# Up-bias table folded over both halves of the partitions: pairs of 64-row matmuls instead of 128-row ones

## The chip, the cores and the metric

The kernel runs on one core of one Trainium2 chip. The metric is the device time of one execution in microseconds (us). Before the change it is 1502.85 us, the median of 3 runs (1502.51 to 1503.81). One further execution was taken by the profiler. It took 1498.58 us, and all rows below are from it.

## The reference

One layer of a hybrid decoder over 512 prompt rows and 32 sample rows (544 tokens of 1024 features): a pooling and gating mixer, then a mixture of experts, then a gated input embedding and a last norm. The change touches the mixture of experts only, and in it the two biases:

```python
logits = (x @ w_router + b_router).astype(jnp.float32)
top_logit, top_idx = lax.top_k(logits, TOP_K)          # 4 of 32 experts
...
def expert_block(args):
    xe, e = args                                       # 128 rows, one expert
    gu = xe @ w_up[e] + b_up[e]                        # 1024 -> 2048
    glu = jnp.minimum(gu[:, :D_FF], SWIGLU_LIMIT)
    lin = jnp.clip(gu[:, D_FF:], -SWIGLU_LIMIT, SWIGLU_LIMIT)
    act = glu * jax.nn.sigmoid(SWIGLU_ALPHA * glu) * (lin + 1.0)
    return act @ w_down[e] + b_down[e]                 # 1024 -> 1024
```

`b_up` is 32 experts by 2048, `b_down` 32 by 1024.

## The kernel before

The program is written out engine by engine, with semaphores between the engines and no scheduler: the order on each engine is the order of the code. It has three stages. The first (to about 249 us) does the mixer, the router and the tables. The second is a loop over experts, one step per expert block of 128 rows. The third (from about 1394 us) adds the expert rows, does the embedding gate and the last norm.

In the expert loop each step reads 12 MB of weights: 8 chunks of `w_up` and 4 of `w_down`, 1 MB each, through a ring of 6 buffers (`raw`) that SP fills. The arithmetic is in float32r, and accuracy comes from splitting: ACT copies each chunk to a rounded high part (`w_hi`, line 822), DVE subtracts to get the low part (`w_lo`, line 1466), and TensorE multiplies high by high, high by low and low by high. So each chunk is 12 matmuls of 128 rows by 512 columns: 8 in `hi_products` (line 1161) and 4 in `lo_products` (line 1170).

The biases are added by TensorE as well, in `bias` (line 1151), which opens each accumulation. The table `bias_hl` holds for each expert the high part of its bias in partition e and the low part in partition 32+e; columns 0 to 2047 are `b_up`, 2048 to 3071 are `b_down`, and partitions 64 to 127 are zero. The stationary operand (`oh_up` or `oh_dn`, 128 by 128) is one in the two partitions of the step's expert and zero elsewhere. It comes from `bias_row`, which holds the expert number that each partition stands for. A matmul of the two writes the bias into all 128 rows of PSUM. The up bias is 4 matmuls of 512 columns (`up_start`, line 1181), the down bias 2 (`dn_start`, line 1207). Both stand between matmuls that use all 128 rows: the up bias between the last `lo_products` of the step before and the first `hi_products` of `w_up`; the down bias between a `lo_products` and the first `hi_products` of `w_down`.

The table is made once, in the first stage: 4 DMAs from ACT's queue into `bias_raw` (lines 773 and 774), ACT's copy (line 783), DVE's subtraction (line 1460) and POOL's clearing of partitions 64 to 127 (line 653). TensorE waits for it before the first `x_transposes` of the loop.

Of the kernel before, what the change touches and what calls it, by code (L numbers as in the profile page):

```python
# [22 lines left out]
F32 = mybir.dt.float32  # L23
F32R = mybir.dt.float32r
I32 = mybir.dt.int32
U32 = mybir.dt.uint32
ALU = mybir.AluOpType
ACT = mybir.ActivationFunctionType
AX = mybir.AxisListType

P = 128
# [9 lines left out]
def build(nc, x_prompt, x_sample, state_pool, p_prompt, p_sample, norm_mix, w_in, w_pool, pool_scale,  # L41
# [3 lines left out]
    SEQ, D = x_prompt.shape[1:]  # L45
# [13 lines left out]
    E = w_router.shape[2]  # L59
    FF = w_down.shape[2]  # L60
# [17 lines left out]
    with ctx:  # L78
        def sb(name, shape, dt=F32, scope=ctx):
            return scope.enter_context(nc.sbuf_tensor(name, shape, dt))  # L80

        def sem(name):
            return ctx.enter_context(nc.semaphore(name))
# [19 lines left out]
        bias_row = sb("bias_row", [P, 1])  # L103
# [1 line left out]
        with ExitStack() as s:  # L105
            xTh = sb("xTh", [P, KD, T], F32R, scope=s)
        with ExitStack() as s:
            bias_hl = sb("bias_hl", [P, 2 * FF + D], F32R, scope=s)
        gate_hi3 = sb("gate_hi3", [P, 2, D], F32R)
        junk_t = sb("junk_t", [P, D])  # L110
        x_rows = sb("x_rows", [P, D])
# [3 lines left out]
        with ExitStack() as s:  # L115
            xTl = sb("xTl", [P, KD, TT * P], F32R, scope=s)
        with ExitStack() as s:
            bias_raw = sb("bias_raw", [P, 2 * FF + D], scope=s)
        ple = sb("ple", [P, TT, D])
        with ExitStack() as s:  # L120
            w_v_sb = sb("w_v_sb", [P, KD, SG], scope=s)
# [95 lines left out]
        with ExitStack() as s:  # L217
# [12 lines left out]
            oh_up = sb("oh_up", [P, P], F32R, scope=s)  # L230
            oh_dn = sb("oh_dn", [P, P], F32R, scope=s)
# [45 lines left out]
        JOBS += [(("over", 0), "V"), (("ple", LAST), "A")]  # L277
        assert TT == 5 and all(n % 4 != 3 for n in range(len(JOBS) - 2, len(JOBS)))
        JOB = {name: n for n, (name, _) in enumerate(JOBS)}
        EMPTIED = {}  # L280
        for n, (name, who) in enumerate(JOBS):
            EMPTIED[name] = sum(w == who for _, w in JOBS[:n + 1])
        TOTAL = {who: sum(w == who for _, w in JOBS) for who in "AV"}

        s_job = sem("job_filled")
        s_emptied = {"A": sem("job_emptied_act"), "V": sem("job_emptied_dve")}

        def bank(name, b=0):
            return ps[:, 2 * (JOB[name] % 4) + b, :]
# [12 lines left out]
        def job_filled(eng, name):  # L302
            eng.wait_ge(s_job, JOB[name] + 1)

        ld = {n: sem("ld_" + n) for n in (
            "gain w_v w_z w_u small pool_w state sgu ln w_out gain2 router bias ple p gain_f w_out2 w_out3".split())}
        s_x = [sem(f"ld_x_{t}") for t in range(TT)]
        s_ident = sem("ident_made")
        s_const = sem("constants_made")
# [21 lines left out]
        s_bias_hi = sem("bias_hi")  # L331
        s_bias = sem("bias_table")
# [50 lines left out]
        gu = ps[:, 0:4, :].rearrange("p a b -> p (a b)")  # L383
        dn = ps[:, 4:6, :].rearrange("p a b -> p (a b)")
# [180 lines left out]
        def _(pool):  # L565
            chain = [0]

            def link(ins):
                chain[0] += 1
                ins.then_inc(s_pchain, 1)  # L570
                pool.wait_ge(s_pchain, chain[0])
# [41 lines left out]
            for rest in range(NS, P, NS):  # L613
# [2 lines left out]

            link(pool.iota(bias_row[:], pattern=[[0, 1]], base=0, channel_multiplier=1,
                           allow_small_or_imprecise_dtypes=True))
            link(pool.tensor_scalar(bias_row[E:2 * E, :], bias_row[E:2 * E, :], float(E), None, ALU.subtract))
            pool.tensor_scalar(bias_row[2 * E:P, :], bias_row[2 * E:P, :], 1000.0, None, ALU.add).then_inc(s_const, 1)  # L620
            pool.wait_ge(s_const, 13)

            for t in range(TT):
# [6 lines left out]
            for g in range(G):  # L630
# [7 lines left out]
                for i in range(g + 1):  # L638
                    dst = (sumA, sumB)[(g - i) % 2]
                    sh = 1 << i  # L640
                    lo = (2 << i) - 1
# [8 lines left out]
            pool.memset(x_rows[:], 0.0).then_inc(s_xzero, 1)  # L650
            pool.wait_ge(s_xzero, 1)
            pool.wait_ge(s_sum, G)
            pool.memset(bias_hl[2 * E:P, :].bitcast(F32), 0.0).then_inc(s_bias, 1)
            pool.wait_ge(s_bias, 1)

            pool.wait_ge(s_sum, G)
            for t in range(TT):
# [49 lines left out]
        def _(act):  # L707
# [62 lines left out]
            act.wait_ge(s_mix, 2 * G)  # L770
            act.wait_ge(s_out, 16 * STORES)
            for i in range(2):
                act.dma_start(bias_raw[i * E:(i + 1) * E, 0:2 * FF], b_up[0]).then_inc(ld["bias"], 16)
                act.dma_start(bias_raw[i * E:(i + 1) * E, 2 * FF:], b_down[0]).then_inc(ld["bias"], 16)

            def square2(t):
                act.wait_ge(s_emptied["V"], EMPTIED[("out", t)])
# [1 line left out]
                act.activation(junk[:], resid[:, t, :], ACT.Square, accum_out=sq2[:, t:t + 1]).then_inc(s_sq, 1)  # L779

            def bias_high():
                act.wait_ge(ld["bias"], 64)
                act.activation(bias_hl[0:2 * E, :], bias_raw[0:2 * E, :], ACT.Copy).then_inc(s_bias_hi, 1)

            def p_transposed(t):
                job_filled(act, ("pT", t))
# [133 lines left out]
        def _(pe):  # L920
# [90 lines left out]
            for g in range(G):  # L1011
# [11 lines left out]
                for t in range(LAST):  # L1023
                    pe.matmul(bank(name)[:, t * P:(t + 1) * P], v_sb[:, t, g * P:(g + 1) * P], wsT[:, g, :], start=True, stop=True)
                pe.matmul(bank(name, 1)[:, 0:NS], v_sb[0:NS, LAST, g * P:(g + 1) * P], block_w[0:NS, g, :],
                          start=True, stop=True).then_inc(s_job, 1)
# [16 lines left out]
            for i in range(TT + 2):  # L1043
                if i < TT:
# [3 lines left out]
                    for ks in w_z_halves:  # L1048
                        for b in range(2):
                            for k in range(ks.start, ks.stop):  # L1050
                                if i == 0 and b == 0:
# [4 lines left out]
                                    if k == 3 * KD // 4:  # L1056
# [4 lines left out]
                                               skip_group_check=True)  # L1061
# [45 lines left out]
            for k in range(TOPK):  # L1107
                pe.wait_ge(s_picks, k + 1)
                for t in range(TT):
                    mm = pe.matmul(bank(name)[:, 0:E], picks[:, k % 2, t, :], chosen_row[:, t, k, :],  # L1110
                                   start=(k == 0 and t == 0), stop=(k == TOPK - 1 and t == LAST))
# [34 lines left out]
                    mm = pe.transpose(tp[:, k * P:(k + 1) * P], lin[:, k * P:(k + 1) * P], ident[:])  # L1146
                mm.then_inc(s_atp, 1)

            def bias(out, oh, lo, hi):
                for c in range(lo, hi, 512):  # L1150
                    pe.matmul(out[:, c - lo:c - lo + 512], oh[:], bias_hl[:, c:c + 512], start=True, stop=False,  # L1151
                              skip_group_check=True)

            def hi_products(J, s, out, parts):

# [18 lines left out]
            def up_start(u):  # L1174
                pe.wait_ge(s_xhi, u + 1)
                pe.wait_ge(s_xlo, u + 1)
                pe.wait_ge(s_oh, u + 1)
                if not (isinstance(u, int) and u == 0):
                    pe.wait_ge(s_lin, u)
                    pe.wait_ge(s_glu, u)  # L1180
                bias(gu, oh_up, 0, 2 * FF)

            def up_args(c):
                return gu, [(xT_hi[:, c, :], xT_lo[:, c, :], 0, 2 * FF)]
# [16 lines left out]
            def dn_start(u):  # L1201
                pe.wait_ge(s_ahi, u + 1)
                pe.wait_ge(s_alo, u + 1)
                pe.wait_ge(s_oh, u + 2)
                if not (isinstance(u, int) and u == 0):
                    pe.wait_ge(s_y, u)
                bias(dn, oh_dn, 2 * FF, 2 * FF + D)

            def step(J, has_dn=True):  # L1210
# [74 lines left out]
        def _(dve):  # L1285
            chain = [0]

            def link(ins):
                chain[0] += 1
                ins.then_inc(s_chain, 1)  # L1290
                dve.wait_ge(s_chain, chain[0])
# [127 lines left out]
            def logits_top(t):  # L1419

                name = ("logits", t)
                job_filled(dve, name)
                dve.tensor_copy(logits[:, t, :], bank(name)[:, 0:E]).then_inc(s_emptied["V"], 1)
                dve.wait_ge(s_emptied["V"], EMPTIED[name])
                link(dve.max(top8[:, t, :], logits[:, t, :]))
                link(dve.max_index(top_i[:, t, :], top8[:, t, :], logits[:, t, :]))
                dve.tensor_scalar(neg_max[:, t:t + 1], top8[:, t, 0:1], -1.0, None, ALU.mult).then_inc(s_top, 1)
                link(dve.tensor_copy(top_f[:, t, :], top_i[:, t, 0:TOPK]))
                link(dve.tensor_tensor(chosen[:, t, :, :],
                                       expert_iota[:].rearrange("p (o e) -> p o e", o=1).to_broadcast([P, TOPK, E]),  # L1430
                                       top_f[:, t, :].rearrange("p (k o) -> p k o", o=1).to_broadcast([P, TOPK, E]),
                                       ALU.is_equal))
                dve.tensor_reduce(mask[0:NT[t], t, :], chosen[0:NT[t], t, :, :].rearrange("p k e -> p e k"), AX.X,
                                  ALU.add).then_inc(s_mask, 1)
# [3 lines left out]
            for i in range(TT + 2):  # L1438
                if i < TT:
                    name = ("out", i)  # L1440
                    job_filled(dve, name)
                    for b in range(2):
                        x = resid[0:NT[i], i, b * 512:(b + 1) * 512]
                        ins = dve.tensor_tensor(x, x, bank(name, b)[0:NT[i], :], ALU.add)  # L1444
                    ins.then_inc(s_emptied["V"], 1)
                if 0 <= i - 2 < TT:
                    logits_top(i - 2)
                if i < TT:
                    dve.wait_ge(s_sq, TT + i + 1)
                    dve.tensor_scalar(var2[:, i:i + 1], sq2[:, i:i + 1], 1.0 / D, NORM_EPS, ALU.mult, ALU.add).then_inc(s_var, 1)  # L1450
                    dve.wait_ge(s_rstd, TT + i + 1)
                    if i >= 2:
                        job_filled(dve, ("h2T", i - 2))
                        dve.wait_ge(s_xrow[i - 2], 16)
                    dve.scalar_tensor_tensor(out=xn[:, i % 2, :], in0=resid[:, i, :], scalar=rstd2[:, i:i + 1], in1=gain2[:],
                                             op0=ALU.mult, op1=ALU.mult).then_inc(s_xn, 1)
                if i == 2:

                    dve.wait_ge(s_bias_hi, 1)
                    dve.tensor_tensor(bias_hl[E:2 * E, :], bias_raw[E:2 * E, :], bias_hl[E:2 * E, :].bitcast(F32),  # L1460
                                      ALU.subtract).then_inc(s_bias, 1)
            def lo_part(J, s):

                wait_split_used(dve, s_lused, J, s)
                wait_hi(dve, J, s)
                dve.tensor_tensor(w_lo[:, s % SPLIT, :], raw[:, s % RING, :], w_hi[:, s % SPLIT, :].bitcast(F32),  # L1466
                                  ALU.subtract).then_inc(s_lo, 1)
# [266 lines left out]
```

## Time and profile before

| what | value |
|---|---|
| median of 3 runs | 1502.85 us |
| profiled execution | 1498.58 us |
| its span, first to last instruction | 1496.8 us |
| TensorE busy | 1442.8 us, 96% |
| VectorE busy | 1224.3 us, 82% |
| ScalarE busy | 926.8 us, 62% |
| mean granted clock of TensorE | 0.980 of full |

### The profile page before, as it was taken

Reading aid. Unit: us, or ns where it says so; the run is one execution under the profiler, and the core shown is the slowest. Engines: PE = TensorE matmul, PEld = TensorE weight load, DVE = VectorE, ACT = ScalarE, POOL = GpSimd, SP = SyncE. Lnnn points to the kernel's source line nnn. Section 1 sums busy time; section 2 is a strip of 40 time slices with the busy share of each in tenths; the row PEclk is TensorE's granted clock in tenths of the full one; section 3 lists DMA queues with packets and bytes.
Section 4 is the critical chain, followed back from the end, with each engine's and each line's share of the span. In section 5 each row is a group of like instructions: output and inputs, shape, how many; then the busy total and the mean of one; then the engine's idle time right before and its main releaser. Section 6 shows DMA issues by size and latency. Waiting matters only on the chain.

```text
span 1496.8 us, 19576 instructions
## 1 busy us (share of the span) xinstructions
PE 1442.8 (96%) x6625; PEld 1156.2 (77%) x6625; DVE 1224.3 (82%) x1001; ACT 926.8 (62%) x628; POOL 218.1 (15%) x130
## 2 busy tenths in 40 slices
PE   6999999899999999999999999999999999999497
PEld 3794466788888888888888888888888888888385
DVE  3742346899999999999999999999999999999774
ACT  4311133677777777777777777777777777777322
POOL 3131000011111111111111111111111111111100
PEclk9999988999999999999999999999999999999788
DMA  8016033899999999999999999999999999999641
GB/s 306 1 60 204 30 144 106 306 350 369 373 374 369 368 361 362 367 363 363 360 369 367 360 365 364 377 362 366 372 373 368 372 368 373 366 368 350 240 155 44
DMA packets 93818, 457.16 MB, mean 305 GB/s; under 512 B 13132, under 2 KB 14704, under 8 KB 59863
## 3 DMA queue, kind: packets, MB, share of 16 engines
q1 hardware_dynamic: 83953, 437.48, 76.5%
q0 software_dynamic: 9360, 17.85, 3.2%
q10 hardware_dynamic: 478, 1.47, 0.4%
q8 instruction: 17, 0.28, 0.1%
q14 instruction: 10, 0.08, 0.0%
HBM read 451.61 MB, written 21.58 MB: 316 GB/s over the span
## 4 chain that ended last, share of the span: by engine, by line
PE 94%; DMA 2%; DVE 2%; issue 1%; ACT 1%; SPq 0%; DVEq 0%; POOLq 0%; POOL 0%; ACTq 0%
PE ps L1161 46%; PE ps L1170 23%; PE ps L1060 5%; PE ps L1151 3%; PE ps L936 2%; PE ps L1146 2%; PE ps L1139 2%; PE ps L1039 2%; PE ps L982 1%; PE ps L984 1%; PE ps L991 1%; PE ps L422 1%; PE ps L424 1%; PE ps L431 1%; DMA expert_rows<-y_rows,scatter_col 1%
## 5 line engine op out<-in xcount | busy, mean ns | idle before, releaser
L1466 DVE TENSOR_TENSOR w_lo<-raw,w_hi 128x2048 fp32r<-128x2048 f32 x384 | 868.0, 2287 | 60.5 <-PE ps L1170 57.4
L822 ACT ACTIVATE w_hi<-raw 128x2048 fp32r<-128x2048 f32 x384 | 732.1, 1916 | 234.1 <-PE ps L1161 189.9
L1161 PE MATMUL ps<-w_hi,xT_hi 128*128 128x512 f32 x1024 | 277.3, 393 | 0.0
L1170 PE MATMUL ps<-w_lo,xT_hi 128*128 128x512 f32 x1024 | 274.2, 390 | 0.0
L1161 PE MATMUL ps<-w_hi,xT_lo 128*128 128x512 f32 x1024 | 274.1, 390 | 0.0
L1161 PEld LDWEIGHTS ps<-w_hi,xT_lo 128*128 128x128 f32 x1024 | 192.4, 188 | 40.4
L1170 PEld LDWEIGHTS ps<-w_lo,xT_hi 128*128 128x128 f32 x1024 | 192.3, 188 | 39.8
L1161 PEld LDWEIGHTS ps<-w_hi,xT_hi 128*128 128x128 f32 x1024 | 190.5, 188 | 37.6
L678 POOL DMA_INDIRECT expert_rows<-y_rows,scatter_col x32 | 145.3, 4542 | 403.7 <-ACT y_rows L856 403.7
L1161 PE MATMUL ps<-w_hi,aT_hi 128*128 128x512 f32 x512 | 140.8, 397 | 0.0
L1170 PE MATMUL ps<-w_lo,aT_hi 128*128 128x512 f32 x512 | 137.1, 390 | 0.4 <-DVE w_lo L1466 0.4
L1161 PE MATMUL ps<-w_hi,aT_lo 128*128 128x512 f32 x512 | 137.2, 390 | 0.0
L1161 PEld LDWEIGHTS ps<-w_hi,aT_lo 128*128 128x128 f32 x512 | 96.6, 189 | 20.2
L1170 PEld LDWEIGHTS ps<-w_lo,aT_hi 128*128 128x128 f32 x512 | 96.0, 188 | 20.6 <-DVE w_lo L1466 0.8
L670 POOL DMA_INDIRECT x_rows<-xn_rows,gather_col x30 | 30.5, 1016 | 556.5 <-PE ps L1139 524.0
L1161 PEld LDWEIGHTS ps<-w_hi,aT_hi 128*128 128x128 f32 x512 | 94.5, 189 | 18.0
L856 ACT ACTIVATE y_rows<-ps 128x1024 f32<-128x1024 f32 x32 | 32.9, 1028 | 72.1 <-PE ps L1170 72.1
L1572 DVE TENSOR_SCALAR glu<-ps 128x1024 f32<-128x1024 f32 x32 | 39.2, 1225 | 29.8 <-PE ps L1170 29.8
L779 ACT ACTIVATE junk<-resid 128x1024 f32<-128x1024 f32 x5 | 5.3, 1057 | 69.2 <-DVE resid L1444 69.2
L1444 DVE TENSOR_TENSOR resid<-resid,ps 128x512 f32<-128x512 f32 (+1 forms) x10 | 6.4, 682 | 48.2 <-PE ps L1060 48.2
L1151 PE MATMUL ps<-bias_hl,oh_up 128*128 128x512 f32 x128 | 35.3, 399 | 5.2 <-DVE xT_lo L1562 4.1
L1562 DVE TENSOR_TENSOR xT_lo<-ps,xT_hi 128x1024 fp32r<-128x1024 f32 x33 | 40.2, 1218 | 0.0
(229 smaller groups left out, 1294.2 us busy)
## 6 DMA issues: line engine op xcount, KB each, us to landing
raw<-in_w_up_dram SPq DMA_DIRECT2D x256, 1024.0 KB, 6.4
raw<-in_w_down_dram SPq DMA_DIRECT2D x128, 1024.0 KB, 7.6
raw<-expert_rows SPq DMA_DIRECT2D x8, 1024.0 KB, 7.8
raw<-in_w_ple_gate_dram SPq DMA_DIRECT2D x4, 1024.0 KB, 5.3
resid<-in_x_prompt_dram SPq DMA_DIRECT2D x4, 512.0 KB, 10.2
w_v_sb<-in_w_in_dram SPq DMA_DIRECT2D x2, 1024.0 KB, 9.4
w_z_sb<-in_w_in_dram SPq DMA_DIRECT2D x2, 1024.0 KB, 13.0
w_u_sb<-in_w_in_dram SPq DMA_DIRECT2D x2, 1024.0 KB, 8.4
```

The lines of the kernel that those rows point to most:

```text
L670: pool.indirect_dma_start(x_rows[:], None, xn_dram[:, :], bass.IndirectOffsetOnAxis(ap=col, axis=0), bounds_check=last_token, oob_is_err=F ...
L678: pool.indirect_dma_start(y4_dram[:, :], bass.IndirectOffsetOnAxis(ap=scatter_col[:, 0:1], axis=0), y_rows[:], None, bounds_check=last_row ...
L822: act.activation(w_hi[:, s % SPLIT, :], raw[:, s % RING, :], ACT.Copy).then_inc(s_hi, 1)
L856: act.activation(y_rows[:], dn, ACT.Copy).then_inc(s_y, 1)
L936: mm = pe.matmul(bank(name), xT[:, k, t * P:(t + 1) * P], w_v_sb[:, k, :], start=(k == 0), stop=(k == KD - 1))
L1060: mm = pe.matmul(bank(name, b)[0:n, :], rows_k, w, start=(k == 0), stop=(k == KD - 1), skip_group_check=True)
L1151: pe.matmul(out[:, c - lo:c - lo + 512], oh[:], bias_hl[:, c:c + 512], start=True, stop=False, skip_group_check=True)
L1161: mm = pe.matmul(out[:, c:c + 512], (xh, xl)[xs], w_hi[:, s % SPLIT, base + c:base + c + 512], start=False, stop=False, skip_group_check=True)
L1170: mm = pe.matmul(out[:, c:c + 512], xh, w_lo[:, s % SPLIT, base + c:base + c + 512], start=False, stop=last and k == len(parts) - 1, skip_ ...
L1466: dve.tensor_tensor(w_lo[:, s % SPLIT, :], raw[:, s % RING, :], w_hi[:, s % SPLIT, :].bitcast(F32), ALU.subtract).then_inc(s_lo, 1)
L1562: dve.tensor_tensor(xT_lo[:].rearrange("p k n -> p (k n)"), tp, xT_hi[:].rearrange("p k n -> p (k n)").bitcast(F32), ALU.subtract).then_in ...
L1572: dve.tensor_scalar(glu[:], gu[:, 0:FF], LIMIT, None, ALU.min).then_inc(s_glu, 1)
```

## The change

The table becomes 2048 columns wide. Partitions 0 to 63 hold the high and low parts of the first 1024 columns of `b_up`, partitions 64 to 127 those of the last 1024 columns; `b_down` follows in partitions 0 to 63 only. `bias_row` now names an expert in every partition, so the one-hot operand has a one in each group of 32. The up bias is still 4 matmuls of 512 columns, but each uses 64 rows of the array: the first and third the lower half, the second and fourth the upper half, and the two of a pair write different PSUM banks. The down bias is still 2 matmuls, now with 64 rows, both on the lower half. In the built program the 128-row matmuls carry a tile size of 128 by 128, these six 64 by 128. The loads of the table become 6 DMAs, ACT's copy becomes two, DVE's subtraction two, and POOL no longer clears the upper half.

```diff
-            bias_hl = sb("bias_hl", [P, 2 * FF + D], F32R, scope=s)
+            bias_hl = sb("bias_hl", [P, FF + D], F32R, scope=s)
+            sb("unused_bias", [P, FF], scope=s)
...
-            link(pool.tensor_scalar(bias_row[E:2 * E, :], bias_row[E:2 * E, :], float(E), None, ALU.subtract))
-            pool.tensor_scalar(bias_row[2 * E:P, :], bias_row[2 * E:P, :], 1000.0, None, ALU.add).then_inc(s_const, 1)
+            for g in range(1, 3):
+                link(pool.tensor_scalar(bias_row[g * E:(g + 1) * E, :], bias_row[g * E:(g + 1) * E, :], float(g * E), None, ALU.subtract))
+            pool.tensor_scalar(bias_row[3 * E:P, :], bias_row[3 * E:P, :], float(3 * E), None, ALU.subtract).then_inc(s_const, 1)
...
-            pool.memset(bias_hl[2 * E:P, :].bitcast(F32), 0.0).then_inc(s_bias, 1)
-            pool.wait_ge(s_bias, 1)
...
-                act.dma_start(bias_raw[i * E:(i + 1) * E, 0:2 * FF], b_up[0]).then_inc(ld["bias"], 16)
-                act.dma_start(bias_raw[i * E:(i + 1) * E, 2 * FF:], b_down[0]).then_inc(ld["bias"], 16)
+                for h in range(2):
+                    act.dma_start(bias_raw[(2 * h + i) * E:(2 * h + i + 1) * E, 0:FF],
+                                  b_up[0][:, h * FF:(h + 1) * FF]).then_inc(ld["bias"], 16)
+                act.dma_start(bias_raw[i * E:(i + 1) * E, FF:], b_down[0]).then_inc(ld["bias"], 16)
...
-                act.activation(bias_hl[0:2 * E, :], bias_raw[0:2 * E, :], ACT.Copy).then_inc(s_bias_hi, 1)
+                act.activation(bias_hl[:, 0:FF], bias_raw[:, 0:FF], ACT.Copy)
+                act.activation(bias_hl[0:2 * E, FF:], bias_raw[0:2 * E, FF:], ACT.Copy).then_inc(s_bias_hi, 1)
...
-            def bias(out, oh, lo, hi):
-                for c in range(lo, hi, 512):
-                    pe.matmul(out[:, c - lo:c - lo + 512], oh[:], bias_hl[:, c:c + 512], start=True, stop=False,
-                              skip_group_check=True)
+            def bias(out, oh, at, parts):
+                for c in range(0, FF, 512):
+                    for h in range(parts):
+                        rows = slice(h * 2 * E, (h + 1) * 2 * E)
+                        pe.matmul(out[:, h * FF + c:h * FF + c + 512], oh[rows, :], bias_hl[rows, at + c:at + c + 512],
+                                  start=True, stop=False, skip_group_check=True)
...
-                bias(gu, oh_up, 0, 2 * FF)
+                bias(gu, oh_up, 0, 2)
...
-                bias(dn, oh_dn, 2 * FF, 2 * FF + D)
+                bias(dn, oh_dn, FF, 1)
...
+                    dve.tensor_tensor(bias_hl[3 * E:P, 0:FF], bias_raw[3 * E:P, 0:FF], bias_hl[3 * E:P, 0:FF].bitcast(F32),
                                       ALU.subtract).then_inc(s_bias, 1)
```

TensorE, around the down bias of a loop step, before (`oh_dn` is the one-hot operand; the row of a register instruction only forms a wait's value):

```order
L1161 MATMUL ps<-w_hi,xT_lo 128x512 x4
L1170 MATMUL ps<-w_lo,xT_hi 128x512 x4
L1151 MATMUL ps<-bias_hl,oh_dn 128x512 x2
L391 REGISTER_ALU
L1161 MATMUL ps<-w_hi,aT_hi 128x512 x4
L1161 MATMUL ps<-w_hi,aT_lo 128x512 x4
```

and now, with the changed kernel's line numbers:

```order
L1166 MATMUL ps<-w_hi,xT_lo 128x512 x4
L1175 MATMUL ps<-w_lo,xT_hi 128x512 x4
L1156 MATMUL ps<-bias_hl,oh_dn 128x512 x2
L392 REGISTER_ALU
L1166 MATMUL ps<-w_hi,aT_hi 128x512 x4
L1166 MATMUL ps<-w_hi,aT_lo 128x512 x4
```

Nothing moved: on TensorE the order, the number of matmuls and their outputs are the same, at the up bias too. What differs is how many rows of the array the `bias_hl` matmuls use, which these rows do not show.

POOL, at the end of the mixer, before (`sumA` and `sumB` are window sums, `rstd` the norms' scales that DVE waits for):

```order
L642 TENSOR_TENSOR sumB<-sumA 128x681
L642 TENSOR_TENSOR sumA<-sumB 128x673
L650 MEMSET x_rows 128x1024
L653 MEMSET bias_hl 64x3072
L659 TENSOR_TENSOR rstd<-var,half_neg 128x1 x5
```

and now:

```order
L644 TENSOR_TENSOR sumB<-sumA 128x681
L644 TENSOR_TENSOR sumA<-sumB 128x673
L652 MEMSET x_rows 128x1024
L659 TENSOR_TENSOR rstd<-var,half_neg 128x1 x5
L670 DMA x_rows<-xn_rows,token_of 128x1024 x3
```

The clearing of the table's upper half is gone, and the first `rstd` no longer stands behind it.

## Rows read from the trace of the kernel before

**Rows 1.** Page, part 1: busy us, share of the span, instructions.

```profile
PE 1442.8 (96%) x6625; PEld 1156.2 (77%) x6625; DVE 1224.3 (82%) x1001; ACT 926.8 (62%) x628; POOL 218.1 (15%) x130
```

**Rows 2.** Windows: stretch, length, engines' busy us, PEclk, DMA share, GB/s.

```profile
800.00:1000.00 200.00, 200.00 (x931) 166.67 (x930) 185.84 (x124) 146.55 (x91) 30.73 (x12) 1.00 0.95 365
```

**Rows 3.** TensorE's waits: total us, times, longest.

```profile
PE ps L1151 <- DVE xT_lo L1562: 4.1, 1, 4.1
PE ps L1151 <- DVE aT_lo L1567: 2.5, 1, 2.5
```

**Rows 4.** Timeline of TensorE in the loop: start, us, instruction.

```profile
801.95 0.62 PE L1151 MATMUL ps<-bias_hl,oh_dn 128*128 128x512 f32 x2
...
813.27 1.07 PE L1170 MATMUL ps<-w_lo,aT_hi 128*128 128x512 f32 x4
814.18 1.07 PE L1151 MATMUL ps<-bias_hl,oh_up 128*128 128x512 f32 x4
815.08 1.07 PE L1161 MATMUL ps<-w_hi,xT_hi 128*128 128x512 f32 x4
...
837.75 0.62 PE L1151 MATMUL ps<-bias_hl,oh_dn 128*128 128x512 f32 x2
```

**Rows 5.** Line 1151: ns min/median/max, first and last start.

```profile
L1151 PE MATMUL ps<-bias_hl,oh_up x128: 388/389/764, 248.7 to 1351.9; 128*128 128x512 f32 x128
...
L1151 PE MATMUL ps<-bias_hl,oh_dn x64: 388/389/763, 300.8 to 1392.9; 128*128 128x512 f32 x64
```

**Rows 6.** Timeline of matmuls, a 32-row pair before float32r.

```profile
106.47 0.40 PE L1025 MATMUL ps<-block_w,v_sb 32*128 32x32 f32 x2
106.80 0.40 PE L982 MATMUL ps<-xTh,w_u_hi 128*128 128x272 f32 x1
107.03 0.29 PE L984 MATMUL ps<-xTh,w_u_lo 128*128 128x272 f32 x1
107.16 0.29 PE L982 MATMUL ps<-xTh,w_u_hi 128*128 128x272 f32 x1
```

**Rows 7.** Timeline of the weight loads in that stretch.

```profile
106.46 0.29 PEld L1025 LDWEIGHTS ps<-block_w,v_sb 32*128 32x128 f32 x2
106.80 0.19 PEld L982 LDWEIGHTS ps<-xTh,w_u_hi 128*128 128x128 f32 x1
106.91 0.19 PEld L984 LDWEIGHTS ps<-xTh,w_u_lo 128*128 128x128 f32 x1
```

**Rows 8.** Timeline of matmuls, a 32-row pair before 512 columns.

```profile
115.00 0.40 PE L1025 MATMUL ps<-block_w,v_sb 32*128 32x32 f32 x2
115.33 0.70 PE L1060 MATMUL ps<-w_out_a,ext 128*128 128x512 f32 x1
```

**Rows 9.** Timeline, 32-column float32 stream, then a 128-column load.

```profile
188.39 3.17 PE L1060 MATMUL ps<-w_out_b,uT 128*32 128x512 f32 x7
...
190.11 1.45 PE L1060 MATMUL ps<-w_out_b,uT 128*32 128x512 f32 x3
...
191.49 0.43 PEld L1072 LDWEIGHTS ps<-ident,p_sb 128*128 128x128 f32 x4 [0.84 <-issue]
```

**Rows 10.** Timeline of matmuls, 32-column transposes before float32r.

```profile
80.88 0.60 PE L1006 MATMUL ps<-ident,new_cols 128*32 128x128 f32 x4
81.23 0.37 PE L982 MATMUL ps<-xTh,w_u_hi 128*128 128x272 f32 x1
```

**Rows 11.** Timeline of the first stage, other engines, their idle in brackets.

```profile
32.75 0.23 POOL L620 TENSOR_SCALAR bias_row<-bias_row 64x1 f32<-64x1 f32 x1
...
55.35 5.17 DVE L1403 TENSOR_TENSOR xTl<-xT,xTh 128x544 fp32r<-128x544 f32 x8 [4.17 <-PE ps L936]
...
130.79 1.06 ACT L779 ACTIVATE junk<-resid 128x1024 f32<-128x1024 f32 x1 [17.03 <-DVE resid L1444]
...
132.30 0.56 POOL L659 TENSOR_TENSOR rstd<-var,half_neg 128x1 f32<-128x1 f32 x1 [15.47 <-DVE var L1450]
...
174.64 1.28 DVE L1444 TENSOR_TENSOR resid<-resid,ps 128x512 f32<-128x512 f32 x2 [6.71 <-PE ps L1060]
```

More of the change, by code:

```diff
@@ L117, in build @@
         with ExitStack() as s:
-            bias_raw = sb("bias_raw", [P, 2 * FF + D], scope=s)
+            bias_raw = sb("bias_raw", [P, FF + D], scope=s)
         ple = sb("ple", [P, TT, D])
@@ L781, in bias_high @@
             def bias_high():
-                act.wait_ge(ld["bias"], 64)
-                act.activation(bias_hl[0:2 * E, :], bias_raw[0:2 * E, :], ACT.Copy).then_inc(s_bias_hi, 1)
+                act.wait_ge(ld["bias"], 96)
+                act.activation(bias_hl[:, 0:FF], bias_raw[:, 0:FF], ACT.Copy)
+                act.activation(bias_hl[0:2 * E, FF:], bias_raw[0:2 * E, FF:], ACT.Copy).then_inc(s_bias_hi, 1)
             def p_transposed(t):
@@ L1460, in _ @@
                     dve.tensor_tensor(bias_hl[E:2 * E, :], bias_raw[E:2 * E, :], bias_hl[E:2 * E, :].bitcast(F32),
+                                      ALU.subtract).then_inc(s_bias, 1)
+                    dve.tensor_tensor(bias_hl[3 * E:P, 0:FF], bias_raw[3 * E:P, 0:FF], bias_hl[3 * E:P, 0:FF].bitcast(F32),
                                       ALU.subtract).then_inc(s_bias, 1)
```

## The prediction

> **What bounds the kernel now.** I read the page's busy times first: TensorE is at 96% of the span, no other engine over 82% [rows 1]. Then windows inside the expert loop: in a stretch of 200 us TensorE is busy for all 200, at full granted clock, VectorE for 185.84, ScalarE for 146.55, and the DMA engines for 0.95 of it [rows 2]. So in the loop nothing makes TensorE wait, and VectorE, the next, has 14 us of 200 to spare. TensorE's list of waits says the same of the bias line: of all its matmuls two waited for VectorE, both at the ends of the loop, 4.1 and 2.5 us [rows 3]. A step is 35.80 us (the distance between two down biases) [rows 4]. In it TensorE's time is additive: what a step's instructions gain or lose there, the span gains or loses, 32 times over (128 up matmuls in fours and 64 down matmuls in twos) [rows 5].
>
> The price of a change. The first stage has matmuls with 32 rows between ones with 128. In [rows 6] a pair with 32 rows ends at 106.47 + 0.40 = 106.87; the first float32r matmul behind it ends at 107.20, that is 0.33 us later; the two after it end at 107.32 and 107.45, 0.12 to 0.13 apart. So the change cost 0.20 us. The loads say why [rows 7]: those of a stream follow each other by 0.11 us (106.80, 106.91), but the first after the pair comes 0.33 us after the pair's first load. It was not slipped under the running matmul; TensorE emptied first, and then the load itself lay open. In [rows 8] the same pair ends at 115.40 and the 512-column matmul behind it at 116.03, 0.63 us later, where this kind follows itself by 0.43 (four records between 188.39 and 190.11 [rows 9]): again 0.20. From a stream of long matmuls the way is the same. The last of [rows 9] starts at 190.11 + 2 x 0.43 = 190.97 and has streamed by 191.40; the load for the next tile size starts at 191.49, 0.09 later. With an open load of 0.11 that makes 0.20 for entering as well. One place speaks against a rule for every tile size: behind transposes of 32 columns the next matmul ends 0.12 us after them, without a gap [rows 10]. There the columns changed, not the rows.
>
> No row has a change between 128 and 64 rows. Bounds for it: 0 (if only 32-row tiles empty the array) and 0.20. I take 0.20, since the row changes seen in a stream all cost that.
>
> The page "TensorEngine Tiling (Array Packing)" of the Trainium skill (Tiling Modes, Key Properties) says that changing the tiling mode drains TensorE, and lists 64 by 128 as a mode. It speaks against this change; the trace agrees for 32 rows, with the 0.20 us above, and does not show 64.
>
> The down bias: two matmuls as before, both on the lower half, nothing beside them: 2 x 0.20 = +0.40 us. Bounds 0 and +0.40, and 0.11 more for the second load if one on the same half cannot lie under the first matmul.
>
> The up bias: two changes, +0.40, and four matmuls whose overlap no row shows. Bounds: both pairs fully side by side, 2 x 0.227 in place of 0.907, so -0.45 + 0.40 = -0.05; one after the other, +0.40, and with three open loads of 0.11, +0.73. Without a price for the changes it would be -0.45. I take the pair as overlapping but each matmul as needing its own load, and loads as coming 0.11 apart [rows 7]. Then the second of a pair trails by 0.11, and the four take 2 x 0.227 + 0.11 = 0.56 in place of 0.907: -0.35 + 0.40 = +0.05.
>
> The rest costs nothing. POOL has one more small operation on `bias_row`, 0.23 us and its wait [rows 11], ahead of a scale that VectorE waits for; VectorE later sits idle for 4.17 us until TensorE is done. POOL's clearing of the table goes, but it sat in front of 15.47 us of idle time. ACT issues two more DMAs ahead of 17.03 us of idle time. VectorE's subtraction becomes two over as many columns, ahead of 6.71 us of idle time. If one of these covers were gone, it would cost well under 1 us, once.
>
> The sum: 32 x (0.40 + 0.05) = 14.4 us, on the profiled execution's 1498.58 us 1513.0. The median of the runs is 4.3 us above that execution, so for the median it is 1502.85 + 14.4 = 1517.3 us; I say 1517. What is late next: nothing new, since a slower TensorE leaves the other engines more slack.
>
> **The rivals.**
>
> Pairs that don't pair: the hardware runs the four one after another, as any matmuls in rows 4. Then both biases lose 0.40 us: 32 x 0.80 = 25.6, so 1528.4 us; loads that lie open as well bring it to 1542 at the most (32 x (0.73 + 0.51) = 39.7). For it: no row shows two matmuls at once. Against it: the two use different rows, different table partitions and different PSUM banks. Chance 0.19.
>
> The seam is free and the pairs run (the other side): a change between 128 and 64 rows does not empty the array, the loads go under as in rows 4, and the up bias falls by 0.35 to 0.45 us. 32 times that is 11.2 to 14.5: 1488 to 1492 us. VectorE's 14 us of slack in 200, 2.5 per step, would cover it. It decides from a price of a change under 0.09 to 0.11 us (0.35 or 0.45 over four). For it: only 32-row tiles are in the trace, and 32-column transposes changed for nothing [rows 10]. Against it: both of the row changes shown cost 0.20. Chance 0.12.
>
> The page "TensorE: Matmul & The Clock Gate" of the Trainium skill (Part 3: Packing small matmuls, The mechanism) gives a span of one matmul plus about 4 ns per further tile for matmuls on different row groups. Taken alone it is this rival, at 14.5 us less than before; no run here shows it yet.
>
> Half a seam: the down bias, whose two matmuls sit on the lower half from row 0, joins the stream without emptying it, and only the up bias pays. Then 32 x 0.05 = 1.6 us: 1504.5, no change that can be measured. For it: nothing in the rows; against it: the 32-row pair of rows 6 starts at row 0 as well and pays. Chance 0.07.
>
> **How the numbers follow.** Forecast, 1509 to 1522 us with its bounds (32 x 0.35 = 11.2 on top of the profiled execution or the median, up to an open load in each bias): 0.62. Pairs that don't pair: 0.19. Free seam: 0.12. Half a seam: 0.07. Of this kernel a difference of 0.2%, 3 us, can be told from none. So faster 0.12, within it 0.07, slower 0.81. The range takes in the forecast and the serial pairs and leaves out the two rivals below, and the open loads above: 1507 to 1530.
>
> **What would show it.** Between the last 128-row matmul and the first of a bias, and again behind it, the load should start about 0.09 us after the stream ends, so that matmul ends there lie 0.20 us further apart than in a stream; four times per step. The down bias should take 0.85 us from stream to stream instead of 0.45, the up bias about 0.96 instead of 0.91, and starts in an up pair should lie about 0.11 apart, not 0.227. A step should be 36.25 us instead of 35.80. The forecast is wrong if the loads of the bias lie under the matmuls ahead as before; if up starts lie 0.227 apart, the pairs don't pair. If the step grows by less than its seams, some engine other than TensorE had set it.

## The result, and the profile after

The changed kernel takes 1514.51 us (median of 4 runs, 1513.21 to 1515.07), the one before, timed beside it, 1502.68 (4 runs, 1502.16 to 1503.81). The ratio is 1.0079, with a 95% interval of 1.0063 to 1.0095: slower, by 11.8 us. The profiled execution took 1514.71 us, its span 1513.0.

The page's busy times, in the columns of [rows 1]:

```profile
PE 1458.1 (96%) x6625; PEld 1134.1 (75%) x6625; DVE 1224.3 (81%) x1002; ACT 926.1 (61%) x629; POOL 215.9 (14%) x130
```

TensorE runs the same 6625 matmuls and is busy for 15.3 us more. VectorE is busy for as long as before. The window inside the expert loop, in the columns of [rows 2]:

```profile
800.00:1000.00 200.00, 200.00 (x918) 160.90 (x917) 182.97 (x125) 145.60 (x89) 29.71 (x11) 1.00 0.95 366
```

TensorE is still never idle, at full granted clock, but it gets through 918 matmuls in 200 us instead of 931. Now the timeline of TensorE in one step, in the columns of [rows 4], from a down bias over an up bias to the next down bias:

```profile
810.99 1.07 PE L1175 MATMUL ps<-w_lo,xT_hi 128*128 128x512 f32 x4
811.99 0.73 PE L1156 MATMUL ps<-bias_hl,oh_dn 64*128 64x512 f32 x2
812.65 1.20 PE L1166 MATMUL ps<-w_hi,aT_hi 128*128 128x512 f32 x4
...
823.64 1.07 PE L1175 MATMUL ps<-w_lo,aT_hi 128*128 128x512 f32 x4
824.64 0.73 PE L1156 MATMUL ps<-bias_hl,oh_up 64*128 64x512 f32 x4
825.30 1.20 PE L1166 MATMUL ps<-w_hi,xT_hi 128*128 128x512 f32 x4
826.34 1.08 PE L1166 MATMUL ps<-w_hi,xT_lo 128*128 128x512 f32 x4
...
848.20 0.73 PE L1156 MATMUL ps<-bias_hl,oh_dn 64*128 64x512 f32 x2
```

The step is 848.20 - 811.99 = 36.21 us, 0.41 more than in [rows 4]. Over 32 steps that is 13.1 us.

Read two things here. First, the four matmuls of the up bias take as long as the two of the down bias, 0.73 us. So two did run beside two. Narrow windows around the first pair show it: one of its matmuls alone takes 0.49 us, both together 0.50.

```profile
824.64 0.49 PE L1156 MATMUL ps<-bias_hl,oh_up 64*128 64x512 f32 x1
...
824.64 0.50 PE L1156 MATMUL ps<-bias_hl,oh_up 64*128 64x512 f32 x2
```

Second, the two biases cost the same in all: from the end of the last 128-row matmul ahead to the end of the first one behind. A narrow window gives that first one behind each:

```profile
812.65 0.50 PE L1166 MATMUL ps<-w_hi,aT_hi 128*128 128x512 f32 x1
...
825.30 0.50 PE L1166 MATMUL ps<-w_hi,xT_hi 128*128 128x512 f32 x1
```

Down: 813.15 - 812.06 = 1.09 us. In the stream of before it was three slots of 0.227 (a slot is the distance between two ends in the stream), so 0.68: +0.41. Up: 825.80 - 824.71 = 1.09, before five slots, 1.13: -0.04. A seam also leaves a little behind it: the four matmuls at 825.30 end at 826.50, 0.70 after the first of them, where three slots make 0.68. So -0.04 + 0.41, and about 0.02 behind each bias, make the 0.41.

The weight loads there, in the same columns, idle time of the loading side in brackets:

```profile
811.99 0.29 PEld L1156 LDWEIGHTS ps<-bias_hl,oh_dn 64*128 64x128 f32 x2 [0.35 <-issue]
...
824.64 0.30 PEld L1156 LDWEIGHTS ps<-bias_hl,oh_up 64*128 64x128 f32 x4 [0.35 <-issue]
825.30 0.30 PEld L1166 LDWEIGHTS ps<-w_hi,xT_hi 128*128 128x128 f32 x2 [0.36 <-issue]
```

Ahead of each bias and behind it the loads stop for 0.35 us and start together with the matmul they serve. In the stream they lay under the matmuls ahead. Four loads of the up bias take as long (0.30) as two of the down bias (0.29). The waits answer to [rows 3]:

```profile
PE ps L1156 <- DVE xT_lo L1569: 4.1, 1, 4.1
PE ps L1156 <- DVE aT_lo L1574: 2.5, 1, 2.5
```

They have not grown: the loss is inside TensorE. And line 1156, for [rows 5]:

```profile
L1156 PE MATMUL ps<-bias_hl,oh_up x128: 392/428/494, 253.0 to 1368.2; 64*128 64x512 f32 x128
...
L1156 PE MATMUL ps<-bias_hl,oh_dn x64: 392/428/494, 305.0 to 1409.6; 64*128 64x512 f32 x64
```

From the first up bias to the last down bias it is 1156.6 us; in [rows 5] it was 1144.2. That is 12.4 of the 16.2 us between the two spans (the stretch holds 30 whole steps, 30 x 0.41 = 12.4, and a part of a step at either end; the two parts come out even). The first bias also starts 4.3 us later, and that is not the change. Windows of the stretch ahead of the loop, for the kernel before, the changed one, and two of the experiments below (e2 has the changed first stage, e3 that of before), in the columns of [rows 2]. The kernel before:

```profile
190.00:250.00 60.00, 54.51 (x238) 36.53 (x237) 31.03 (x75) 18.72 (x29) 2.86 (x3) 0.80 0.32 116
```

the changed one:

```profile
190.00:250.00 60.00, 55.60 (x232) 36.44 (x230) 29.26 (x74) 17.71 (x28) 2.85 (x3) 0.75 0.32 116
```

e2:

```profile
190.00:250.00 60.00, 54.50 (x239) 35.49 (x238) 31.12 (x75) 18.73 (x29) 2.86 (x3) 0.80 0.31 116
```

and e3:

```profile
190.00:250.00 60.00, 55.61 (x232) 36.14 (x231) 29.05 (x74) 17.72 (x28) 2.86 (x3) 0.76 0.32 114
```

The granted clock is 0.80 of full speed in the first and third, 0.75 and 0.76 in the others. It follows the execution, not the kernel, and the first bias follows it: 248.7 and 248.6 us in the first and third, 253.0 and 253.2 in the others. Not all of the 4.3 us is the clock's: up to 190 us it is at full speed in all four, and VectorE's copy of the router's logits starts at 160.82 us before and at 161.87 in the changed kernel. That 1 us goes with the execution too (160.67 in e2, 162.09 in e3). Executions of one kernel differ by up to 5 us (those of before beside e1: 1498.83 to 1503.80), so steps, not spans, are compared below.

### The profile page after: what moved, and what is told of

Same layout as the page of the kernel before. It is cut to its first block, busy times and chain, and to the rows that moved or that the text cites. A ratio compares the mean times of both kernels' runs of the same rounds, so it can differ in the third digit from the quotient of the medians.

```text
span 1513.0 us, 19580 instructions
## 1 busy us (share of the span) xinstructions
PE 1458.1 (96%) x6625; PEld 1134.1 (75%) x6625; DVE 1224.3 (81%) x1002; ACT 926.1 (61%) x629; POOL 215.9 (14%) x130
## 4 chain that ended last, share of the span: by engine, by line
PE 94%; DMA 2%; DVE 2%; issue 1%; ACT 1%; SPq 0%; DVEq 0%; POOLq 0%; POOL 0%; ACTq 0%
PE ps L1166 46%; PE ps L1175 23%; PE ps L1063 5%; PE ps L1156 3%; PE ps L939 3%; PE ps L1149 2%; PE ps L1142 2%; PE ps L1042 2%; PE ps L985 1%; PE ps L987 1%; PE ps L994 1%; PE ps L423 1%; PE ps L425 1%; PE ps L432 1%; DMA expert_rows<-y_rows,scatter_col 1%
## 5 line engine op out<-in xcount | busy, mean ns | idle before, releaser
L1166 PE MATMUL ps<-w_hi,xT_hi 128*128 128x512 f32 x1024 | 281.7, 397 | 0.0
L1166 PE MATMUL ps<-w_hi,aT_hi 128*128 128x512 f32 x512 | 143.9, 403 | 0.0
L1166 PEld LDWEIGHTS ps<-w_hi,aT_hi 128*128 128x128 f32 x512 | 91.4, 188 | 27.3 <-issue 11.6
L939 PE MATMUL ps<-w_v_sb,xT 128*128 128x512 f32 x80 | 38.2, 634 | 2.0 <-DMA w_v_sb<-in_w_in_dram 1.7
## 6 DMA issues: line engine op xcount, KB each, us to landing
w_z_sb<-in_w_in_dram SPq DMA_DIRECT2D x2, 1024.0 KB, 13.1
```

The source lines that it names most:

```text
L939: mm = pe.matmul(bank(name), xT[:, k, t * P:(t + 1) * P], w_v_sb[:, k, :], start=(k == 0), stop=(k == KD - 1))
L1166: mm = pe.matmul(out[:, c:c + 512], (xh, xl)[xs], w_hi[:, s % SPLIT, base + c:base + c + 512], start=False, stop=False, skip_group_check=True)
```

## The experiments

The theory after the result: each change between 128 and 64 rows costs 0.20 us, whatever lies between; the up bias gets it back from its pairs, the down bias has nothing to get it back from. Steps are the distance between two down biases, medians over the loop; "up" and "down" stand for the time from the end of the last 128-row matmul ahead to the end of the first behind (before: 1.13 and 0.68).

**e1, only the down bias undone.** The down bias takes all 128 rows again; the upper half of its columns is cleared.

```diff
-                bias(dn, oh_dn, FF, 1)
+                for c in range(0, D, 512):
+                    pe.matmul(dn[:, c:c + 512], oh_dn[:], bias_hl[:, FF + c:FF + c + 512], start=True, stop=False, ...)
```

> The changed kernel with the down bias back on 128 rows (the table's upper half is cleared below it); the up pairs stay. My theory, a price per change of tile size: the two changes around the down bias go, and with them 0.41 us for the seams and about 0.02 us of the stream's recovery behind them, 32 times: a step of 35.78 us, about 1501 to 1503 us, no different from the kernel before. Rival, the loss sits in the up pairs (their overlap is poor or they disturb the stream): the step stays near 36.2 us and the time near 1514 us.

Measured: 1500.41 us (11 runs), ratio 0.9993 (0.9982 to 1.0003); step 35.79. The timeline, two down biases and the up bias between:

```profile
801.56 0.62 PE L1215 MATMUL ps<-bias_hl,oh_dn 128*128 128x512 f32 x2
...
813.88 0.73 PE L1158 MATMUL ps<-bias_hl,oh_up 64*128 64x512 f32 x4
814.54 1.20 PE L1168 MATMUL ps<-w_hi,xT_hi 128*128 128x512 f32 x4
...
837.35 0.62 PE L1215 MATMUL ps<-bias_hl,oh_dn 128*128 128x512 f32 x2
```

The up bias still stands in pairs, and the whole loss is gone (the time is 0.6 us under the range that I expected, less than executions of one kernel differ by). It was the two seams of the down bias; the up bias on its own is worth 0.01 us per step.

**e2, the order within the up bias.** Lower, lower, upper, upper instead of lower, upper, lower, upper.

```diff
-                for c in range(0, FF, 512):
-                    for h in range(parts):
+                for h in range(parts):
+                    for c in range(0, FF, 512):
```

> The changed kernel with the four up matmuls in another order: both of the lower half first, then both of the upper half. Seams and matmuls are the same. My theory, two neighbours in the queue run together when they use different halves: now only the second and third do, so the four take three slots of 0.227 us instead of two; a step of 36.44 us, 7.3 us over the changed kernel, about 1522 us. Rival, a 64-row matmul is simply cheaper or the array takes any two halves it finds further ahead: 36.21 us and 1514 us as before. Other rival, neighbours must alternate strictly: four slots, 36.67 us and 1529 us.

Measured: 1514.55 us (4 runs), ratio 1.0084 (1.0068 to 1.0101); step 36.22, up 1.10. My expectation failed: I had thought that a matmul pairs only with its neighbour in the program. The four again take what two take:

```profile
821.67 0.74 PE L1156 MATMUL ps<-bias_hl,oh_up 64*128 64x512 f32 x4
822.34 1.20 PE L1166 MATMUL ps<-w_hi,xT_hi 128*128 128x512 f32 x4
```

So an upper matmul starts although a lower one, ahead of it in the program, still waits for the lower half: two on one half do not start together, as e3 shows next. e8 takes this further.

**e3, the seams without pairs.** The table of before; all six bias matmuls of a step on the lower 64 rows.

```diff
-                    pe.matmul(out[:, c - lo:c - lo + 512], oh[:], bias_hl[:, c:c + 512], ...)
+                    pe.matmul(out[:, c - lo:c - lo + 512], oh[0:2 * E, :], bias_hl[0:2 * E, c:c + 512], ...)
```

> The kernel before, its table and everything else as it was, but all six bias matmuls of a step use only the lower 64 rows of the array (the upper half of its table is zero). No pairs, only seams: four changes of tile size per step. My theory: 0.41 us for each bias and 0.05 us of recovery: a step of 36.66 us instead of 35.80, 27.5 us more, about 1530 us. Rival, 64 rows are a cheap change and the loss of the changed kernel comes from its table or its pairs: 35.8 us, 1503 us.

Measured: 1531.35 us (4 runs), ratio 1.0183 (1.0164 to 1.0203); step 36.69, up 1.56, down 1.09.

```profile
819.79 0.73 PE L1151 MATMUL ps<-bias_hl,oh_dn 64*128 64x512 f32 x2
...
832.45 1.20 PE L1151 MATMUL ps<-bias_hl,oh_up 64*128 64x512 f32 x4
833.57 1.20 PE L1161 MATMUL ps<-w_hi,xT_hi 128*128 128x512 f32 x4
...
856.49 0.73 PE L1151 MATMUL ps<-bias_hl,oh_dn 64*128 64x512 f32 x2
```

Four on one half take 1.20 us, four on two halves 0.73. This is what "pairs don't pair" would have cost, 3 us above the 1528.4 that the prediction gave that rival. Later loads on the same half lie under the matmuls ahead: the four cost 0.43 more than in a stream, the two of the down bias 0.41, so it is the two seams and hardly more.

**e6, the table alone.** The changed table, its loads and row numbers, and all six matmuls on 128 rows. The up bias then adds both halves' columns, so these biases are not the reference's. POOL clears the upper half under the down bias, as in e1.

```diff
-                        rows = slice(h * 2 * E, (h + 1) * 2 * E)
+                        rows = slice(0, P)
```

> The changed kernel's folded table, loads, copies and row numbers, but all six bias matmuls with 128 rows; this adds the biases of both halves of the columns to each other, so the up bias is not the reference's. My theory: the first stage hides all that the table costs, and the loop is that of before: a step of 35.80 us, 1501 to 1504 us. Rival, the new loads or copies delay the loop: the first bias begins later by the delay, and the time is above 1505 us with an unchanged step.

Measured: 1502.39 us (12 runs), ratio 0.9998 (0.9987 to 1.0009); step 35.80, as before. The edits in the first stage cost nothing that can be measured.

**e4, more changes.** The kernel before, with the four up matmuls on 64, 128, 64 and 128 rows: four changes of size around and within the up bias, none at the down bias.

```diff
+                    rows = slice(0, 2 * E if lo == 0 and (c // 512) % 2 == 0 else P)
-                    pe.matmul(out[:, c - lo:c - lo + 512], oh[:], bias_hl[:, c:c + 512], ...)
+                    pe.matmul(out[:, c - lo:c - lo + 512], oh[rows, :], bias_hl[rows, c:c + 512], ...)
```

> The kernel before with only the first and third of the four up matmuls on the lower 64 rows, the second, the fourth and the down bias on 128. So there are two runs of 64 rows per step, as in the run with all six on the lower half, and four changes of tile size, but both inside the up bias and each run one matmul long. My theory, the price is per change, whatever stands between: a step of 36.65 to 36.70 us as there, 28 us more than before, about 1530 us. Rival, the price is per bias (once for each place where the stream is left): 36.25 us, 1517 us. Other rival, the price grows with the number of 64-row matmuls (two instead of six): about 36.1 us, 1512 us.

Measured: 1528.14 us (4 runs), ratio 1.0170 (1.0149 to 1.0190); step 36.60. The loads of one up bias, each after a gap of its own:

```profile
833.82 0.18 PEld L1152 LDWEIGHTS ps<-bias_hl,oh_up 64*128 64x128 f32 x1 [0.35 <-issue]
834.25 0.19 PEld L1152 LDWEIGHTS ps<-bias_hl,oh_up 128*128 128x128 f32 x1 [0.25 <-issue]
834.67 0.18 PEld L1152 LDWEIGHTS ps<-bias_hl,oh_up 64*128 64x128 f32 x1 [0.24 <-issue]
835.10 0.19 PEld L1152 LDWEIGHTS ps<-bias_hl,oh_up 128*128 128x128 f32 x1 [0.25 <-issue]
835.21 0.42 PEld L1162 LDWEIGHTS ps<-w_hi,xT_hi 128*128 128x128 f32 x2
```

They come 0.42 to 0.43 us apart: a slot of 0.227 and a change of 0.20. The step grew by 0.80, four times 0.20. So the price is per change, into 64 rows and out of them alike, and not per bias. The step is 0.05 us under the range that I expected, which had the recovery of the stream in it. Here there is none: behind this bias the starts lie 0.227 us apart at once, where in the changed kernel they lie 0.231 to 0.236 apart at first. Why, no run shows.

**e5, one seam pair per step, and three pairs in it.** The down bias is folded over both halves as well, and the up bias of the next step is moved beside it. The first high products open the sum in place of the up bias, which is added in the middle.

```diff
-                bias(gu, oh_up, 0, 2)
...
-                hi_products(J, s, *up_args(c))
+                hi_products(J, s, *up_args(c), first=(c == 0))
...
-                bias(dn, oh_dn, FF, 1)
+                if up:
+                    bias(gu, oh_up, 0, FF, False)
+                bias(dn, oh_dn, FF, D // 2, True)
```

> The down bias is folded over both halves as well, and the up bias of the next step is added in the middle of its sum, right in front of the down bias, instead of at its start (the first high products open the sum). So a step has one run of 64-row matmuls, three pairs, and two changes instead of four. My theory: from the stream before to the stream behind 1.32 us (1.09 as measured for two pairs and 0.23 for a third), where the six took 1.59 so measured: 0.27 us less, 0.02 back for the recovery, a step of 35.56 us, 7.8 us less than before, about 1494.7 us. Rival, the first low parts or the down bias's waits hold up the moved up bias, or VectorE becomes the bound at the shorter step: TensorE gets waits in the loop and the time is 1500 us or more.

Measured: 1493.97 us (5 runs, 1493.53 to 1495.03), ratio 0.9948 (0.9935 to 0.9961); step 35.56. This beats both kernels. Two successive blocks:

```profile
802.76 0.73 PE L1156 MATMUL ps<-bias_hl,oh_up 64*128 64x512 f32 x4
803.33 0.39 PE L1156 MATMUL ps<-bias_hl,oh_dn 64*128 64x512 f32 x2
803.65 1.19 PE L1166 MATMUL ps<-w_hi,aT_hi 128*128 128x512 f32 x4
...
837.31 1.07 PE L1175 MATMUL ps<-w_lo,xT_hi 128*128 128x512 f32 x4
838.31 0.73 PE L1156 MATMUL ps<-bias_hl,oh_up 64*128 64x512 f32 x4
838.88 0.40 PE L1156 MATMUL ps<-bias_hl,oh_dn 64*128 64x512 f32 x2
839.21 0.50 PE L1166 MATMUL ps<-w_hi,aT_hi 128*128 128x512 f32 x1
```

From the stream's end to the first end behind it is 839.71 - 838.38 = 1.33 us (median 1.32) where six matmuls in a stream make seven slots, 1.59. Three slots saved are 0.68, two changes cost 0.40, and 0.27 is left; the step keeps 0.24 of it.

**e7, the move alone.** The kernel before with the same move, on 128 rows.

```diff
-                bias(gu, oh_up, 0, 2 * FF)
...
+                if up:
+                    bias(gu, oh_up, 0, 2 * FF, start=False)
                 bias(dn, oh_dn, 2 * FF, 2 * FF + D)
```

> The kernel before with the same move of the up bias next to the down bias, but the old table and 128 rows throughout. My theory: the order of matmuls in a full stream costs nothing, a step of 35.80 us, 1501 to 1504 us; so the gain of the version with one pair of changes would come from its pairs. Rival, the move itself gains (the step starts without the bias's wait) or loses: more than 0.1 us per step, 3 us, either way.

Measured: 1502.56 us (12 runs), ratio 0.9998 (0.9989 to 1.0007); step 35.80, the block of six bias matmuls 1.59 as in a stream. So e5's gain is the pairs', not the move's.

**e8, how far ahead.** e5 with three lower matmuls first (up, up, down), then the three upper ones in the same order.

```diff
-                if up:
-                    bias(gu, oh_up, 0, FF, False)
-                bias(dn, oh_dn, FF, D // 2, True)
+                for h in range(2):
+                    if up:
+                        bias(gu, oh_up, 0, FF, False, (h,))
+                    ...
```

> The version with one pair of changes, its six 64-row matmuls in another order: the three of the lower half first, then the three of the upper half. After the run in which two of one half came before two of the other and all four still took two slots, the theory is that a matmul can start ahead of earlier ones that wait for the other half. If it can pass two of them, as it passed one, the block stays at 1.32 us and the step at 35.56 us. Rival, it passes one at most: the third of the lower half and the first of the upper meet, and the block takes at least one slot more, 1.55 us and a step of 35.79 us; rival, starts are in order, and the earlier run had another reason: two slots more, 1.77 us and 36.01 us.

Measured: 1496.09 us in one run, beside 1502.20 for the kernel before, also in one; what counts here is the step, 35.56, as in e5.

```profile
837.74 0.74 PE L1156 MATMUL ps<-bias_hl,oh_up 64*128 64x512 f32 x4
838.30 0.40 PE L1156 MATMUL ps<-bias_hl,oh_dn 64*128 64x512 f32 x2
838.64 0.50 PE L1166 MATMUL ps<-w_hi,aT_hi 128*128 128x512 f32 x1
```

The rows stand in order of start. All four up matmuls start ahead of both down matmuls, though in the program a down matmul is third. So in this kernel TensorE does not start these matmuls in program order: an upper one passes two lower ones that wait. How many it can pass was not tried further.

## Why the prediction was right

**The bound.** TensorE is the loop's only limit and its time is additive: the step grew by 0.41 us, and the loop from first to last bias by 12.4. In it no wait for another engine grew; behind the loop's last bias one did, once, for a low part (`w_lo`), from 0.4 to 1.3 us. This held.

**The price of a change, 0.20 us.** It was taken over from other tiles, as no row showed 64. For leaving a tile [rows 6] and [rows 8] are changes of rows. For entering, [rows 9] is not: there 128 rows stay and 32 columns become 128, and [rows 10], with the same change of columns, shows no gap. So this half of the price came out right from a row that did not bear on it, which is luck. A row that does stands in the trace before, right above those of [rows 7], the loads ahead of the 32-row pair:

```profile
106.04 0.30 PEld L1024 LDWEIGHTS ps<-wsT,v_sb 128*128 128x128 f32 x2
```

Two loads in 0.30 us, 0.19 for the last, lie 0.11 apart, so the second starts at 106.15; the first on 32 rows, at 106.46, starts 0.31 later, 0.20 more than in the stream. For 64 rows the price held to the hundredth: the down bias grew by 0.41 for two changes (predicted 0.40), and e4's four gave 0.80. So did its make-up. The load behind a 128-row stream was expected 0.09 us after the stream's end: the last matmul starts at 824.32 (the fourth of the row at 823.64, three slots later), streams for 0.227, and the load starts 0.09 after that. The down bias, "0.85 us from stream to stream", is 0.86. The Trainium skill's page "TensorEngine Tiling (Array Packing)" (Tiling Modes, Key Properties) says that changing the tiling mode drains TensorE; the trace agrees for 64 rows, with this 0.20 us.

**The up bias, +0.05 us.** This is the term that was mis-sized. It measured -0.04 (-0.02 with what the stream loses behind it). The step that failed is "each matmul as needing its own load, and loads as coming 0.11 apart": [rows 7], from which it came, shows loads on the same rows. Loads on two halves run side by side, as the matmuls do; four take 0.30 us, as two do. The starts of a pair lie 3 to 4 ns apart, where I expected 0.11 us. The lower bound in the prediction, -0.05, was the true case. The same section of the Trainium skill says that different tiles can load weights and multiply in parallel, and the page "TensorE: Matmul & The Clock Gate" (Part 3: Packing small matmuls, The mechanism) gives about 4 ns per further tile; the trace agrees with both, and the prediction had used the second for the free seam alone.

**What was left out.** The matmuls behind a seam start some ns further apart for a while: 0.02 us per bias, 0.05 per step. By luck it took back half of what the up bias did better than its term. So the step came out at 36.21 us, not 36.25.

**The first stage.** Free, as predicted (e6).

**The sum.** 32 x 0.41 = 13.1 us instead of 14.4; 1517 was 2.5 us too high. The other 1.2 us lie within what executions of one kernel differ by. The forecast's upper bound, 1522, is not what its terms give: 0.11 more in each bias makes 32 x 0.67 = 21.4 us, so 1520.0 on the profiled execution and 1524.3 on the median. Nothing hangs on it.

**The rivals.** Pairs that don't pair: false here, and realised in e3 at 1531.35 us (the prediction: 1528.4). The free seam and half a seam: false, since both biases pay twice; the down bias, which starts at row 0, pays in full. The pair's gain that the free seam spoke of was there, 0.45 us per step, and the up bias's own two changes ate 0.40 of it.

## What to carry to other kernels

Price a change of row tiling as two seams per visit: here 0.40 us, against 0.227 saved per pair of 512-column matmuls. By that arithmetic one pair loses (not run); two broke even here and three gained 0.24 us per step, so gather all small matmuls of a step in one block, moving an addition to the middle of a sum if need be, and leave alone (on full rows) whatever has no partner. A term of a sum that a trace prices only for one case (loads on the same rows) is not a price for the other (loads on different rows): keep both ends, and look which the change makes.

## What the runs showed of the hardware that was not expected

- TensorE looks past a waiting matmul. With the lower half's matmuls queued first, those of the upper half still ran beside them: step 36.22 against 36.21 us (e2), 35.56 against 35.56 (e8), where the third in the program started behind the fourth and fifth. The second start of a pair comes 3, 7 and 10 ns behind the first (medians of the changed kernel, e2 and e8), where it is the second, third and fourth in the program. That would fit a hand-out in program order, about 3 ns each (an estimate from these three), to two halves that then work on their own; no run tells this from a search ahead.
- Weight loads on two halves start 4 ns apart and run side by side; on the same rows they come 0.11 us apart at best [rows 7].
- A change of rows costs the same 0.20 us with 64 rows as with 32, in either direction. Each bias of the changed kernel leaves about 0.02 us more behind it in the stream; e4's up bias left none.
